# Expert units of layer 0 cut into quarters of 32 rows: 43 units in place of 49

## The chip, the cores and the metric

The kernel runs on one core of a Trainium2 chip. The metric is the time of one execution on the device in microseconds (us), the median of three timed runs. The engines are named as in the profile: PE is TensorE (matmuls), PEld its weight loads, DVE VectorE, ACT ScalarE, POOL GpSimd, SP SyncE; SPq, POOLq and so on are their queues, which issue the transfers.

## What is computed

A two-layer block for 256 context tokens and 256 image tokens with 1024 features. Each layer has a mixer (attention, an mLSTM and an RWKV-7 branch, merged by gates) and then a mixture of experts. All of it is float32. The part that the change touches is the mixture of experts:

```python
def moe_ffn(xf, w_router, router_bias, w_e_gate, w_e_up, w_e_down, w_s_gate, w_s_up, w_s_down):
    scores = jax.nn.sigmoid((xf @ w_router).astype(jnp.float32))
    ...                                  # 64 experts in 8 groups; 4 groups, then 8 experts a token
    _, eidx = lax.top_k(masked, TOP_K)
    wts = wts / (wts.sum(-1, keepdims=True) + 1e-20) * ROUTED_SCALE
    routed = routed_experts(xf, eidx, wts, w_e_gate, w_e_up, w_e_down)
    return routed + swiglu(xf, w_s_gate, w_s_up, w_s_down)

def swiglu(h, w_gate, w_up, w_down):     # 1024 -> 256 -> 1024 for a routed expert
    return (jax.nn.silu(h @ w_gate) * (h @ w_up)) @ w_down
```

In layer 0 all 512 tokens go through it, which makes 4096 pairs of token and expert; in layer 1 only the 256 image tokens, 2048 pairs. Routed with the reference's inputs, the busiest experts of layer 0 get 143, 140, 139, 122, 118, 103 and 94 tokens; those of rank 11 to 28 (counted from 0) get 83 down to 61, and those from rank 29 on get 61 down to 27.

## The kernel before

**Units.** The experts are worked through in units of 128 rows. One unit is: its rows are fetched from DRAM by a gather (`fetch` in `px_pool`, L1594), turned by eight 128x128 transposes (`flip_rows`, L1660), multiplied by the gate and up weights in eight steps of 128 features (`gate_up`, L1670, 512 output columns into one bank), passed through the silu on ACT and DVE (L1772, L1848, L1851), turned again (`flip_hidden`, L1676), multiplied by the down weights (`down`, L1685, two halves of two steps) and written back by a scatter (`store`, L1600). On PE the units are interleaved: gate-up of unit u, the turn of the rows of unit u+1, the down product of unit u-1, the turn of the hidden rows of unit u (`px_pe`).

**What a unit holds.** `Plan` (L43) lays the experts, by how many tokens they have, on positions p of a fixed list of units. A letter F is a unit of one expert (128 rows, weights used at full width, a tile of 128x128 in the array). P is a unit of two experts with 64 rows each: `sides` (L1652) then gives two matmuls for each step, one for output rows 0 to 63, one for 64 to 127, each with a tile of 128x64 in the array and with its own weights as the moving operand. D is a further unit for the last pair of experts, so that each of these has 192 rows. Layer 0 has 30 units of the kind F and 19 of two halves, 49 in all; layer 1 has 34, all of two halves. The last unit of each list is done by a loop (`rest_of`), which also takes what does not fit.

**Weights.** An expert's gate and up weights are 2048 KB and its down weights 1024 KB. There are four places for each; position p uses place p mod 4. SP issues the loads (`px_sync`, L1527 and L1530) in a fixed order: the load for position p waits until the last unit that uses position p-4 has done its gate-up, or its down product. `Plan.loads` holds that order. Layer 0 loads its first four experts once the router has named them.

**The router** (`ro_dve`) computes on DVE in a chain of small operations where each pair of token and expert goes: its row in the units, from `Plan.table`, or a row in the loop's extra blocks of 64 rows.

The program prints here the functions that the diff touches.

Of the kernel before, what the change touches and what calls it, by code (L numbers as in the profile page):

```python
# [7 lines left out]
ALU = mybir.AluOpType  # L8
# [5 lines left out]
P = 128  # L14
L = 2
D = 1024
# [3 lines left out]
T = TC + TX  # L20
TT = T // P
# [20 lines left out]
class Plan:  # L42


    def __init__(self, pinned, order):
        units, blocks, wide, doubled, p = [], {p: [] for p in range(E)}, [], [], 0
        for what in order:
            if what == "F":
                blocks[p] += [(len(units), 0), (len(units), 1)]
                units.append((p, p))  # L50
                wide.append(p)
                p += 1
                continue
            if what == "P":
                p += 2
            else:
                doubled += [p - 2, p - 1]
            blocks[p - 2].append((len(units), 0))
            blocks[p - 1].append((len(units), 1))
            units.append((p - 2, p - 1))  # L60
        assert p == E and units[-1] == (E - 2, E - 1)
        self.pinned, self.all, self.units = pinned, units, units[:-1]
        self.n = len(units) + NOV // 2 + 1
        first = list(range(pinned))
        for some in (doubled, wide, range(E)):
            first += [q for q in some if q not in first]
        self.by_rank, self.blocks = first, blocks
        self.three = any(len(v) > 2 for v in blocks.values())
        last_use = [max(n for n, unit in enumerate(units) if q in unit) for q in range(E)]
        loads = [(last_use[q - 4] + late, last_use[q - 4], kind, q) for q in range(4, E - 2) for kind, late in (("gate_up", 0), ("down", 1.3))]  # L70
        self.loads = [x[1:] for x in sorted(loads, key=lambda x: x[0])]

    def table(self, q):

        v = [P * unit + 64 * half for unit, half in self.blocks[q]]
        return v[0] - P * len(self.all), (v + v[-1:])[1] - v[0], (v[2] - v[1] if len(v) > 2 else 0), len(v)


PLAN = (Plan(0, "FFDP" * 2 + "FFP" * 4 + "P" + "FFP" * 5 + "P" + "FFP" * 4), Plan(4, "PPPDPD" + "P" * 28))
NBLK = max(at.n for at in PLAN)  # L80


# [75 lines left out]
def bcast(ap, axis, n):  # L158

    a = ap.unsqueeze(axis)  # L160
    shape = list(a.shape)
    shape[axis] = n
    return a.broadcast_to(shape)


def build(nc, xin, consts, smalls, wsm, wst, wexp, out):
    es = ExitStack()
    with es:
# [22 lines left out]
        ps = [es.enter_context(nc.psum_tensor(f"bank{i}", [P, 512], F32)) for i in range(8)]  # L191
# [127 lines left out]
        def mod_dve(dve, ch, chunks, bank):  # L319
# [6 lines left out]
            for l, j in chunks:  # L326
                for v, scale in ((0, 8), (1, 32)):
                    if j == scale // 4 + 1:
# [11 lines left out]
                                                      s=32, nm=32, ex=32, pn=32, t=32, pte=32, o=32, oe=4)  # L340
# [954 lines left out]
        def ro_dve(dve, ch, l):  # L1295
            t0 = 0 if l == 0 else TC // P
            n_t = TT - t0
            V = nc.vector
# [42 lines left out]
            at = PLAN[l]  # L1341
            U = len(at.all)
# [6 lines left out]
            ch.link(V.tensor_tensor(r_ties[col, :], r_ties[col, :], cn("before", E)[col, :], ALU.mult))  # L1349
            V.tensor_tensor(r_beats[col, :], r_beats[col, :], r_ties[col, :], ALU.add).then_inc(ro["rk"], 1)  # L1350

            ch.link(V.tensor_scalar(r_pos[:, t0:, :], ps[2][:, t0 * E:TT * E].rearrange("p (t e) -> p t e", e=E), float(P * U), None, ALU.add))
            ch.link(V.tensor_scalar(r_j[:, t0:, :], r_pos[:, t0:, :], 1.0 / BLK, 0.5 / BLK - 0.5 - P * U / BLK, ALU.mult, ALU.add))
            ch.link(V.tensor_scalar(r_j[:, t0:, :], r_j[:, t0:, :], ROUND, None, ALU.add))

            dve.wait_ge(ro["ranked"], l * RO["ranked"] + 1)
            for n in range(4):
# [4 lines left out]
            dve.wait_ge(ro["rk"], l * RO["rk"] + 1)  # L1362
            V.tensor_scalar(r_tab[col, 4, :], ident[col, 0:E], r_n[col, 0:1], None, ALU.mult).then_inc(ro["rk"], 1)
            ch.add(V.tensor_copy(r_incl, ps[3][:, 0:E]))
            ch.link(V.tensor_scalar(r_j[:, t0:, :], r_j[:, t0:, :], ROUND, None, ALU.subtract))
            ch.link(V.scalar_tensor_tensor(r_at[:, t0:, :], r_j[:, t0:, :], -float(BLK), r_pos[:, t0:, :], ALU.mult, ALU.add))

            dve.wait_ge(ro["ranked"], l * RO["ranked"] + 2)
            ch.link(V.tensor_copy(r_row[:, :, :], ps[1][:, 2 * E:7 * E].rearrange("p (a b) -> p a b", b=E)))
            first, second, third, blocks = (r_row[:, n, :] for n in range(4))  # L1370
            dve.wait_ge(ro["rk"], l * RO["rk"] + 2)
            V.tensor_copy(EJI[:, 0:E], r_row[:, 4, :]).then_inc(ro["end"], 1)
            ch.add(V.scalar_tensor_tensor(r_blk[:, t0:, :], r_j[:, t0:, :], 1.0, bcast(second, 1, n_t), ALU.is_ge, ALU.mult))
            ch.link(V.tensor_scalar(r_nov, r_incl, 1.0 / BLK, 0.5 - 0.5 / BLK, ALU.mult, ALU.add))
            ch.add(V.tensor_tensor(r_blk[:, t0:, :], r_blk[:, t0:, :], bcast(first, 1, n_t), ALU.add))
            ch.link(V.tensor_scalar(r_nov, r_nov, ROUND, None, ALU.add))
            if at.three:
                ch.add(V.scalar_tensor_tensor(r_h[:, t0:, :], r_j[:, t0:, :], 2.0, bcast(third, 1, n_t), ALU.is_ge, ALU.mult))
            ch.link(V.tensor_scalar(r_nov, r_nov, ROUND, None, ALU.subtract))
            if at.three:  # L1380
                ch.add(V.tensor_tensor(r_blk[:, t0:, :], r_blk[:, t0:, :], r_h[:, t0:, :], ALU.add))
            ch.link(V.tensor_tensor(r_nov, r_nov, blocks, ALU.subtract))
            ch.add(V.tensor_tensor(r_over[:, t0:, :], r_j[:, t0:, :], bcast(blocks, 1, n_t), ALU.is_ge))
            ch.link(V.tensor_scalar(r_nov, r_nov, 0.0, None, ALU.max))
            ch.add(V.tensor_tensor(r_at[:, t0:, :], r_at[:, t0:, :], r_blk[:, t0:, :], ALU.add))
            ch.link(V.tensor_tensor_scan(out=r_incl, data0=ones[:, 0:E], data1=r_nov, initial=0.0, op0=ALU.mult, op1=ALU.add))
            ch.link(V.tensor_tensor(r_excl, r_incl, r_nov, ALU.subtract))
            ch.link(V.tensor_tensor(r_excl, r_excl, blocks, ALU.subtract))
            ch.link(V.tensor_tensor(r_spill[:, t0:, :], r_j[:, t0:, :], bcast(r_excl, 1, n_t), ALU.add))
            ch.link(V.tensor_scalar(r_h[:, t0:, :], r_spill[:, t0:, :], NOV / 2, 64.0 - P * NOV / 2, ALU.is_ge, ALU.mult))  # L1390
            ch.link(V.scalar_tensor_tensor(r_spill[:, t0:, :], r_spill[:, t0:, :], float(P), r_h[:, t0:, :], ALU.mult, ALU.add))
            ch.link(V.tensor_tensor(r_spill[:, t0:, :], r_spill[:, t0:, :], r_blk[:, t0:, :], ALU.subtract))
# [21 lines left out]
            n = at.n  # L1414
# [231 lines left out]
        def px_pe(pe, l, before):  # L1646
            tiles, at = tiles_of(l), PLAN[l]
            U = len(at.units)
# [2 lines left out]

            def sides(unit):  # L1652

                left, right = unit
                return [(0, P, left)] if left == right else [(0, 64, left), (64, P, right)]

            def flip_rows(s, done, freed=None):
                for h in range(2):
# [32 lines left out]
                flip_rows(u % 4, un["pe"], tl["pe"] if u == U - 1 else None)  # L1691

            def rows_through(u):
                for _, _, p in sides(at.units[u]):
                    pe.wait_ge(gu_in[p % 4], 16 * (loads_past(l, p % 4) + p // 4 + 1))
                if u >= 2:
                    pe.wait_ge(un["dve"], after(l, "dve", "hidden", u - 2))

                def wait_rows(k):
                    if k % 4 == 0:  # L1700
                        eng = ("act", "dve")[k // 4]
                        pe.wait_ge(un[eng], after(l, eng, "rows", u))
                gate_up(at.units[u], u % 2, wait_rows).then_inc(un["pe"], 1)

            def rows_down(u):
                for _, _, p in sides(at.units[u]):
# [17 lines left out]
            rows_down(U - 1)  # L1724

            rest = rest_of(pe, l)
            s, unit = U % 2, (2, 3)
# [466 lines left out]
```

## Time and profile before

| | us |
|---|---|
| median of three runs | 3216.1 |
| lowest and highest | 3215.99, 3217.38 |
| the profiled execution | 3204.1 |
| its span | 3202.2 |
| layer 0, first gate-up to the loop's gate-up | 1132.50 to 1721.31 |
| layer 1, first gate-up to the loop's gate-up | 2626.26 to 3132.42 |

| engine | busy us | share of the span |
|---|---|---|
| PE | 2762.2 | 86% |
| PEld | 1435.7 | 45% |
| DVE | 908.9 | 28% |
| ACT | 624.2 | 19% |
| POOL | 170.7 | 5% |

A row of the timeline says when a run of like instructions starts and how long it takes to the modelled end of the last; the distance from the start of one row to the start of the next is the more exact measure. The chain of waits gives each piece up to the start of the next. PEclk is the granted clock of PE as a share of 2.4 GHz. The program's records count two for each float32 matmul of these shapes, so "x16" is eight matmuls.

### The profile page before, as it was taken

How to read it: one execution, taken by the hardware profiler on the slowest of the kernel's cores; microseconds unless marked ns; L12 is line 12 of the kernel's file. 1: busy time of each engine (PE TensorE's matmuls, PEld its weight loads, DVE VectorE, ACT ScalarE, POOL GpSimd, SP SyncE). 2: the span in 40 equal slices, each digit the busy share in tenths (PEclk: the TensorE clock that was granted, in tenths of full speed). 3: DMA queues.
4: the chain of work that ended last, by engine and by line, in shares of the span. 5: the costliest groups of instructions: out<-in, count | busy, mean ns of one | idle time of the engine just before them, and what ended most of it. 6: DMA issues, size and time to landing. Idle time of an engine off the chain costs nothing.

```text
span 3202.2 us, 38572 instructions
## 1 busy us (share of the span) xinstructions
PE 2762.2 (86%) x15804; PEld 1435.7 (45%) x15804; DVE 908.9 (28%) x1994; ACT 624.2 (19%) x1194; POOL 170.7 (5%) x178
## 2 busy tenths in 40 slices
PE   6868898999999899989898587898989979788885
PEld 3333334765444644434343334343878853233333
DVE  1231454452111622111112412244452142111114
ACT  3231223222001111111110222223222021111111
POOL 0000000000000011111111000000000001111100
PEclk9999568999999699999999699759999979989987
DMA  6000001342210469999996501001223169999994
GB/s 265 33 40 33 0 0 53 134 160 80 79 53 0 190 255 387 418 399 409 370 411 252 232 20 53 33 0 53 82 108 146 65 252 390 424 422 416 415 405 177
DMA packets 74559, 617.37 MB, mean 193 GB/s; under 512 B 17678, under 2 KB 17678, under 8 KB 32016
## 3 DMA queue, kind: packets, MB, share of 16 engines
q1 hardware_dynamic: 50192, 564.52, 43.4%
q0 software_dynamic: 24192, 50.39, 4.2%
q8 instruction: 125, 2.05, 0.3%
q14 instruction: 50, 0.41, 0.0%
HBM read 604.87 MB, written 47.71 MB: 204 GB/s over the span
## 4 chain that ended last, share of the span: by engine, by line
PE 80%; DVE 9%; issue 4%; DMA 3%; ACT 3%; SPq 0%; DVEq 0%; POOLq 0%; ACTq 0%; POOL 0%
PE bank L1670 19%; PE bank L1685 9%; PE bank L1156 8%; PE bank L286 7%; PE bank L356 3%; PE bank L1171 3%; PE bank L1161 3%; PE bank L1660 2%; PE bank L576 2%; PE bank L584 2%; DMA arena<-expert_rows 2%; PE bank L377 1%; PE bank L397 1%; PE bank L874 1%; PE bank L889 1%
## 5 line engine op out<-in xcount | busy, mean ns | idle before, releaser
L1670 PE MATMUL bank<-ring,arena 128*64 128x512 f32 (+1 forms) x1648 | 589.4, 631 | 96.6 <-issue 93.3
L1670 PEld LDWEIGHTS bank<-ring,arena 128*64 128x64 f32 (+1 forms) x1648 | 203.3, 158 | 421.6 <-issue 420.5
L1156 PE MATMUL bank<-normed,ring 128*128 128x512 f32 (+1 forms) x768 | 255.5, 486 | 0.0
L1670 PE MATMUL bank<-branches,arena 128*64 128x512 f32 (+1 forms) x528 | 254.6, 639 | 0.0
L1848 DVE TENSOR_TENSOR arena<-bank,arena 128x256 f32<-128x256 f32 x83 | 35.2, 425 | 702.3 <-ACT arena L1772 702.3
L286 PE MATMUL bank<-normed,ring 128*128 128x512 f32 x512 | 223.4, 598 | 1.3 <-DVE branches L491 1.3
L1594 POOL DMA_INDIRECT arena<-hidden_rows,block_slots x81 | 82.5, 1018 | 2588.8 <-DVE block_slots L1423 1985.3
L1156 PEld LDWEIGHTS bank<-normed,ring 128*128 128x128 f32 x768 | 145.9, 190 | 102.2 <-issue 92.3
L1772 ACT ACTIVATE arena<-bank 128x256 f32<-128x256 f32 x83 | 31.9, 385 | 684.4 <-PE bank L1670 684.4
L1685 PE MATMUL bank<-ring,arena 128*64 128x512 f32 (+1 forms) x560 | 163.4, 597 | 1.3 <-DVE arena L1854 1.3
L286 PEld LDWEIGHTS bank<-normed,ring 128*128 128x128 f32 x512 | 98.0, 192 | 123.9 <-issue 122.1
L1685 PE MATMUL bank<-arena 128*64 128x512 f32 (+1 forms) x528 | 139.9, 604 | 1.1 <-ACT arena L1775 1.1
L1854 DVE COPY arena<-bank 128x512 f32<-128x512 f32 x83 | 57.4, 692 | 223.7 <-PE bank L1685 223.7
L1660 PEld LDWEIGHTS bank<-consts,arena 128*128 128x128 f32 x664 | 73.4, 141 | 64.5 <-issue 59.7
L1600 POOL DMA_INDIRECT expert_rows<-arena,block_slots x81 | 80.7, 996 | 355.9 <-ACT arena L1775 232.5
L356 PE MATMUL bank<-normed,ring 128*128 128x512 f32 x192 | 86.7, 615 | 9.5 <-ACT normed L280 9.5
L1660 PE MATMUL bank<-consts,arena 128*128 128x128 f32 x664 | 89.1, 277 | 5.7 <-DVE arena L1843 3.5
L584 PE MATMUL bank<-arena 128*128 128x256 f32 (+3 forms) x136 | 82.3, 712 | 11.4 <-DVE arena L726 11.0
L1161 PE MATMUL bank<-branches,ring 128*128 128x512 f32 (+1 forms) x256 | 90.4, 486 | 0.0
L1685 PEld LDWEIGHTS bank<-ring,arena 128*64 128x64 f32 (+1 forms) x560 | 55.6, 152 | 77.6 <-issue 77.6
L1670 PEld LDWEIGHTS bank<-branches,arena 128*64 128x64 f32 (+1 forms) x528 | 78.8, 155 | 16.7 <-issue 16.7
L1171 PE MATMUL bank<-arena,ring 128*128 128x512 f32 (+1 forms) x256 | 83.1, 486 | 2.6 <-DVE arena L1200 2.6
(429 smaller groups left out, 3713.1 us busy)
## 6 DMA issues: line engine op xcount, KB each, us to landing
ring<-in_wexp SPq DMA_DIRECT2D x96, 2048.0 KB, 19.3
ring<-in_wst SPq DMA_DIRECT2D x54, 2048.0 KB, 8.5
branches<-in_wexp SPq DMA_DIRECT2D x34, 2048.0 KB, 21.7
ring<-in_wexp SPq DMA_DIRECT2D x66, 1024.0 KB, 21.3
arena<-in_wexp SPq DMA_DIRECT2D x64, 1024.0 KB, 21.8
arena<-expert_rows SPq DMA_DIRECT2D x12, 2048.0 KB, 7.3
ring<-in_wst SPq DMA_DIRECT2D x4, 1536.0 KB, 11.1
hidden_rows<-arena SPq DMA_DIRECT2D x6, 512.0 KB, 2.8
```

Of the source, the lines that this page charges most:

```text
L286: last = nc.tensor.matmul(bank, weights[:, k, j0:j0 + n], H[:, k, :], start=(k == 0), stop=(k == KD - 1))
L356: last = nc.tensor.matmul(ps[j][:, :], w[:, k, (j % 4) * P:(j % 4 + 1) * P], H[:, k, :], start=(k == 0), stop=(k == KD - 1))
L576: nc.tensor.matmul(ps[3 + p % 3][:, j0:j1], zk[q, s * P:(s + 1) * P], zq[q, j0:j1], start=True, stop=True, tile_position=(32 * h, 0)).then ...
L584: nc.tensor.matmul(ps[6 + u % 2][:, j0:j1], VA[:, s, u % MLH, :], Sb[:, p % 2, j0:j1], start=(p in firsts), stop=(p + 1 in firsts or p == ...
L1156: last = nc.tensor.matmul(ps[2 * (n % 4)][:, c0:], wg[:, k, i * P:(i + 1) * P], H[:, k, c0:], start=(k == 0), stop=(k == KD - 1))
L1161: last = nc.tensor.matmul(ps[2 * (n % 4) + 1][:, c0:], wb[:, k, :], BR[:, k, c0:], start=(k == b0), stop=(k == b1 - 1))
L1171: last = nc.tensor.matmul(ps[m % 4][:, c0:], w[:, k, (m % 4) * P:(m % 4 + 1) * P], YM[:, k, c0:], start=(k == 0), stop=(k == KD - 1))
L1594: pool.indirect_dma_start(XG[s], None, hx[l], bass.IndirectOffsetOnAxis(ap=ids_of[:, u, 0:1], axis=0), bounds_check=TOKENS[l] - 1, oob_is_ ...
L1600: pool.indirect_dma_start(yrows[l], bass.IndirectOffsetOnAxis(ap=ids_of[:, u, 1:2], axis=0), YB[s], None, bounds_check=TOKENS[l] * TOPK - ...
L1660: last = nc.tensor.transpose(ps[h][:, k * P:(k + 1) * P], XG[s][:, (4 * h + k) * P:(4 * h + k + 1) * P], ident)
L1670: last = nc.tensor.matmul(ps[2 + s][r0:r1, :], XT_[:, s, k * P + r0:k * P + r1], wt[:, k, :], start=(k == 0), stop=(k == KD - 1))
L1685: last = nc.tensor.matmul(ps[5 + h][r0:r1, :], HDT[:, s, k * P + r0:k * P + r1], wt[:, k, h * 512:(h + 1) * 512], start=(k == 0), stop=(k ...
```

## The change

In `Plan` a unit is now a list of pieces (first row, last row, position), and a piece may have 128, 96, 64 or 32 rows:

- F and P are as before.
- D is two experts in two units: the first has 128 rows in a unit of its own and 32 more (160 in all), the second 96 rows beside those 32.
- T is three experts in two units: 96 rows beside 32, and 96 rows beside 32; the expert in the middle has both pieces of 32 (64 in all).
- Layer 0 is "DPFPT" + "DPPFPT"*3 + "FPT"*2 + "TFP": 43 units, of which 11 have one expert, 14 two halves, and 18 a piece of 96 beside one of 32. By rank there are 4 experts with 160 rows, 7 with 128, 18 with 96 and 35 with 64, 5504 rows in all where there were 6272.
- Layer 1's list gives the same 34 units as before (S stands where D stood).

`sides` cuts a piece of 96 rows into one of 64 and one of 32 for PE, so such a unit has three matmuls for each step: a tile of 128x64 and two of 128x32. The waits for weights go by pieces, the loads by the same rule as before, so that their order follows the new last uses. The router looks up the first row, the rows of the first piece, the jump to the second and the room of each expert, and computes with rows in place of blocks.

```diff
+            elif what == "D":
+                units += [[(0, P, p)], [(0, 96, p + 1), (96, P, p)]]
+                p += 2
+            elif what == "T":
+                units += [[(0, 96, p), (96, P, p + 1)], [(0, 96, p + 2), (96, P, p + 1)]]
+                p += 3
...
-PLAN = (Plan(0, "FFDP" * 2 + "FFP" * 4 + "P" + "FFP" * 5 + "P" + "FFP" * 4), Plan(4, "PPPDPD" + "P" * 28))
+PLAN = (Plan(0, "DPFPT" + "DPPFPT" * 3 + "FPT" * 2 + "TFP"), Plan(4, "PPPSPS" + "P" * 28))
...
             def sides(unit):
 
-                left, right = unit
-                return [(0, P, left)] if left == right else [(0, 64, left), (64, P, right)]
+                return [side for r0, r1, p in unit for side in ([(r0, r0 + 64, p), (r0 + 64, r1, p)] if r1 - r0 == 96 else [(r0, r1, p)])]
```

In the router the three operations on DVE before the rank is known (L1352 to L1354) become one, two more before the table is known (L1365, L1366) go, and the chain behind the table (L1373 to L1394) is written anew: before, 11 operations over all tokens and 8 over the 64 experts in layer 0 (9 and 8 in layer 1); now 17 and 6 in both layers.

```diff
-            ch.link(V.tensor_scalar(r_pos[:, t0:, :], ps[2][:, t0 * E:TT * E].rearrange("p (t e) -> p t e", e=E), float(P * U), None, ALU.add))
-            ch.link(V.tensor_scalar(r_j[:, t0:, :], r_pos[:, t0:, :], 1.0 / BLK, 0.5 / BLK - 0.5 - P * U / BLK, ALU.mult, ALU.add))
-            ch.link(V.tensor_scalar(r_j[:, t0:, :], r_j[:, t0:, :], ROUND, None, ALU.add))
+            ch.link(V.tensor_copy(r_pos[:, t0:, :], ps[2][:, t0 * E:TT * E].rearrange("p (t e) -> p t e", e=E)))
...
+            ch.add(V.tensor_tensor(r_blk[:, t0:, :], r_pos[:, t0:, :], bcast(split, 1, n_t), ALU.is_ge))
+            ch.add(V.tensor_tensor(r_spill[:, t0:, :], r_pos[:, t0:, :], bcast(room, 1, n_t), ALU.subtract))
+            ch.link(V.tensor_tensor(r_nov, r_incl, room, ALU.subtract))
```

On PE, at the second unit of layer 0, before: the turn of the first unit's hidden rows, then the gate-up of unit 1, which is one expert (L1670), the turn of the rows of unit 2 (L1660) and the down product of unit 0 (L1685).

```order
L1676 MATMUL bank4<-consts,arena 128x128 x2
L1670 MATMUL bank3<-ring,arena 128x512 x8
L1660 MATMUL bank0<-consts,arena 128x128 x4
L1660 MATMUL bank1<-consts,arena 128x128 x4
L1685 MATMUL bank5<-ring,arena 128x512 x2
```

The eight full-width matmuls of L1670 stood in one run; the change has another kind of unit in that place.

The same place of the changed program, where the lines are L1671 and L1665; unit 1 is 96 rows of position 1 and 32 of position 0.

```order
L1671 MATMUL bank4<-consts,arena 128x128 x2
L1665 MATMUL bank3<-ring,arena 64x512
L1665 MATMUL bank3<-ring,arena 32x512 x2
L1665 MATMUL bank3<-ring,arena 64x512
L1665 MATMUL bank3<-ring,arena 32x512 x2
```

Each of the eight steps is now one matmul with 64 output rows and two with 32, and the next step's matmul with 64 stands right behind them.

Further on PE, in the changed program, the start of unit 5 (96 rows of position 7, whose weights lie in `branches`, and 32 of position 8): the down product of unit 3, the turn of the hidden rows of unit 4, and two steps of the gate-up.

```order
L1680 MATMUL bank5<-ring,arena 128x512 x2
L1680 MATMUL bank6<-ring,arena 128x512 x2
L1671 MATMUL bank4<-consts,arena 128x128 x2
L1665 MATMUL bank3<-branches,arena 64x512
L1665 MATMUL bank3<-branches,arena 32x512
L1665 MATMUL bank3<-ring,arena 32x512
L1665 MATMUL bank3<-branches,arena 64x512
```

Here too the matmuls alternate between 64 and 32 output rows, the two of 32 being of two experts.

## Rows read from the trace of the kernel before

**Rows 1.** Page: PE's granted clock and DMA over 40 slices of 80 us.

```profile
PEclk9999568999999699999999699759999979989987
GB/s 265 33 40 33 0 0 53 134 160 80 79 53 0 190 255 387 418 399 409 370 411 252 232 20 53 33 0 53 82 108 146 65 252 390 424 422 416 415 405 177
```

**Rows 2.** Chain of waits in order of time, layer 0: start us, us, what.

```profile
1132.50 7.12 PE bank L1670 x16
...
1141.44 6.87 PE bank L1670 x16
...
1362.45 9.68 issue
1372.13 8.83 PE bank L1670 x32
...
1721.31 7.10 PE bank L1670 x32
```

**Rows 3.** Who waited for whom, PE, 1132 to 1722 us: total, times, longest.

```profile
PE bank L1670 <- issue: 21.6, 3, 9.8
```

**Rows 4.** Timeline of PE, three units of layer 0: start us, us, engine, line, what.

```profile
1257.71 0.38 PE L1676 MATMUL bank<-consts,arena 128*128 128x128 f32 x2
1257.93 7.03 PE L1670 MATMUL bank<-ring,arena 128*128 128x512 f32 x16
1264.80 1.04 PE L1660 MATMUL bank<-consts,arena 128*128 128x128 f32 x8
...
1280.80 0.38 PE L1676 MATMUL bank<-consts,arena 128*128 128x128 f32 x2
1281.11 0.64 PE L1670 MATMUL bank<-ring,arena 128*64 128x512 f32 x1
1281.12 0.64 PE L1670 MATMUL bank<-branches,arena 128*64 128x512 f32 x1
...
1288.13 1.09 PE L1660 MATMUL bank<-consts,arena 128*128 128x128 f32 x8
...
1292.71 7.03 PE L1670 MATMUL bank<-ring,arena 128*128 128x512 f32 x16
```

**Rows 5.** Chain of waits, layer 1: a whole unit of two halves.

```profile
2635.18 7.02 PE bank L1670 x32
2643.22 3.58 PE bank L1685 x16
2647.17 7.02 PE bank L1670 x32
```

**Rows 6.** Timeline of PE in layer 0's mLSTM: tiles of 64, 32 and 128 rows.

```profile
376.61 1.91 PE L566 MATMUL bank<-arena,consts 64*128 64x512 f32 x2
378.45 2.07 PE L576 MATMUL bank<-arena 32*128 32x512 f32 x2
380.45 0.80 PE L584 MATMUL bank<-arena 128*128 128x128 f32 x2
381.17 1.64 PE L576 MATMUL bank<-arena 32*128 32x384 f32 x2
...
443.21 1.91 PE L566 MATMUL bank<-arena,consts 64*128 64x512 f32 x2
445.05 2.07 PE L576 MATMUL bank<-arena 32*128 32x512 f32 x2
```

**Rows 7.** Chain of waits, start: a step of the modulation with four groups of 32 columns.

```profile
35.46 1.90 PE bank L303 x16
```

**Rows 8.** A stretch: us, PE busy, granted clock, DMA share, GB/s.

```profile
330.00:345.00 15.00, 15.00 (x21) 0.50 0.00 1
```

**Rows 9.** Timeline of DVE, layer 0: start and end of the chain behind the table.

```profile
1075.51 0.42 DVE L1373 SCALAR_TENSOR_TENSOR arena<-arena 128x256 f32<-128x256 f32 x1
...
1082.16 0.23 DVE L1398 SCALAR_TENSOR_TENSOR arena<-arena 128x64 f32<-128x64 f32 x1
```

**Rows 10.** Page, DMA issues: gate and up weights, KB each, median us to landing.

```profile
ring<-in_wexp SPq DMA_DIRECT2D x96, 2048.0 KB, 19.3
```

More of the change, by code:

```diff
@@ L45, in __init__ @@
     def __init__(self, pinned, order):
-        units, blocks, wide, doubled, p = [], {p: [] for p in range(E)}, [], [], 0
+        units, p = [], 0
         for what in order:
             if what == "F":
-                blocks[p] += [(len(units), 0), (len(units), 1)]
-                units.append((p, p))
-                wide.append(p)
+                units.append([(0, P, p)])
                 p += 1
-                continue
-            if what == "P":
+            elif what == "P":
+                units.append([(0, 64, p), (64, P, p + 1)])
                 p += 2
-            else:
[L57 to L61, printed above, removed]
+            elif what == "D":
[4 more added lines that the diff above has]
+                p += 3
+            else:
+                units.append([(0, 64, p - 2), (64, P, p - 1)])
+        assert p == E and units[-1] == [(0, 64, E - 2), (64, P, E - 1)]
         self.pinned, self.all, self.units = pinned, units, units[:-1]
         self.n = len(units) + NOV // 2 + 1
[L64 to L69, printed above, removed]
+        self.pieces = [[(P * n + r0, r1 - r0) for n, unit in enumerate(units) for r0, r1, q in unit if q == p] for p in range(E)]
+        assert all(len(v) <= 2 for v in self.pieces)
+        self.room = [sum(rows for _, rows in v) for v in self.pieces]
+        self.by_rank = list(range(pinned)) + sorted(range(pinned, E), key=lambda q: -self.room[q])
+        last_use = [max(n for n, unit in enumerate(units) if q in [x[2] for x in unit]) for q in range(E)]
         loads = [(last_use[q - 4] + late, last_use[q - 4], kind, q) for q in range(4, E - 2) for kind, late in (("gate_up", 0), ("down", 1.3))]
@@ L73, in table @@
     def table(self, q):
-        v = [P * unit + 64 * half for unit, half in self.blocks[q]]
-        return v[0] - P * len(self.all), (v + v[-1:])[1] - v[0], (v[2] - v[1] if len(v) > 2 else 0), len(v)
-PLAN = (Plan(0, "FFDP" * 2 + "FFP" * 4 + "P" + "FFP" * 5 + "P" + "FFP" * 4), Plan(4, "PPPDPD" + "P" * 28))
+        (row, rows), *more = self.pieces[q]
+        return row, rows, (more[0][0] - row - rows if more else 0), self.room[q]
+PLAN = (Plan(0, "DPFPT" + "DPPFPT" * 3 + "FPT" * 2 + "TFP"), Plan(4, "PPPSPS" + "P" * 28))
 NBLK = max(at.n for at in PLAN)
@@ L1364, in ro_dve @@
             ch.add(V.tensor_copy(r_incl, ps[3][:, 0:E]))
-            ch.link(V.tensor_scalar(r_j[:, t0:, :], r_j[:, t0:, :], ROUND, None, ALU.subtract))
-            ch.link(V.scalar_tensor_tensor(r_at[:, t0:, :], r_j[:, t0:, :], -float(BLK), r_pos[:, t0:, :], ALU.mult, ALU.add))
             dve.wait_ge(ro["ranked"], l * RO["ranked"] + 2)
             ch.link(V.tensor_copy(r_row[:, :, :], ps[1][:, 2 * E:7 * E].rearrange("p (a b) -> p a b", b=E)))
-            first, second, third, blocks = (r_row[:, n, :] for n in range(4))
+            first, split, jump, room = (r_row[:, n, :] for n in range(4))
@@ L1371, in ro_dve @@
             dve.wait_ge(ro["rk"], l * RO["rk"] + 2)
             V.tensor_copy(EJI[:, 0:E], r_row[:, 4, :]).then_inc(ro["end"], 1)
-            ch.add(V.scalar_tensor_tensor(r_blk[:, t0:, :], r_j[:, t0:, :], 1.0, bcast(second, 1, n_t), ALU.is_ge, ALU.mult))
-            ch.link(V.tensor_scalar(r_nov, r_incl, 1.0 / BLK, 0.5 - 0.5 / BLK, ALU.mult, ALU.add))
-            ch.add(V.tensor_tensor(r_blk[:, t0:, :], r_blk[:, t0:, :], bcast(first, 1, n_t), ALU.add))
-            ch.link(V.tensor_scalar(r_nov, r_nov, ROUND, None, ALU.add))
@@ L1377, in ro_dve @@
[L1377 to L1383, printed above, removed]
@@ L1384, in ro_dve @@
-            ch.link(V.tensor_scalar(r_nov, r_nov, 0.0, None, ALU.max))
+            ch.add(V.tensor_tensor(r_blk[:, t0:, :], r_pos[:, t0:, :], bcast(split, 1, n_t), ALU.is_ge))
+            ch.add(V.tensor_tensor(r_spill[:, t0:, :], r_pos[:, t0:, :], bcast(room, 1, n_t), ALU.subtract))
+            ch.link(V.tensor_tensor(r_nov, r_incl, room, ALU.subtract))
+            ch.add(V.tensor_tensor(r_blk[:, t0:, :], r_blk[:, t0:, :], bcast(jump, 1, n_t), ALU.mult))
+            ch.add(V.tensor_scalar(r_j[:, t0:, :], r_spill[:, t0:, :], 1.0 / BLK, 0.5 / BLK - 0.5, ALU.mult, ALU.add))
@@ L1385, in ro_dve @@
+            ch.link(V.tensor_scalar(r_nov, r_nov, 1.0 / BLK, 0.5 - 0.5 / BLK, ALU.mult, ALU.add))
+            ch.add(V.tensor_tensor(r_at[:, t0:, :], r_pos[:, t0:, :], bcast(first, 1, n_t), ALU.add))
+            ch.add(V.tensor_scalar(r_j[:, t0:, :], r_j[:, t0:, :], ROUND, None, ALU.add))
+            ch.link(V.tensor_scalar(r_nov, r_nov, ROUND, None, ALU.add))
             ch.add(V.tensor_tensor(r_at[:, t0:, :], r_at[:, t0:, :], r_blk[:, t0:, :], ALU.add))
+            ch.add(V.tensor_scalar(r_j[:, t0:, :], r_j[:, t0:, :], ROUND, None, ALU.subtract))
@@ L1386, in ro_dve @@
+            ch.link(V.tensor_scalar(r_nov, r_nov, ROUND, 0.0, ALU.subtract, ALU.max))
+            ch.add(V.tensor_scalar(r_over[:, t0:, :], r_spill[:, t0:, :], 0.0, None, ALU.is_ge))
+            ch.add(V.scalar_tensor_tensor(r_spill[:, t0:, :], r_j[:, t0:, :], -float(BLK), r_spill[:, t0:, :], ALU.mult, ALU.add))
             ch.link(V.tensor_tensor_scan(out=r_incl, data0=ones[:, 0:E], data1=r_nov, initial=0.0, op0=ALU.mult, op1=ALU.add))
-            ch.link(V.tensor_tensor(r_excl, r_incl, r_nov, ALU.subtract))
@@ L1388, in ro_dve @@
[L1388 to L1392, printed above, removed]
+            ch.add(V.tensor_tensor(r_spill[:, t0:, :], r_spill[:, t0:, :], r_at[:, t0:, :], ALU.subtract))
@@ new lines, in ro_dve @@
+            ch.link(V.scalar_tensor_tensor(r_excl, r_incl, float(U), r_nov, ALU.add, ALU.subtract))
+            ch.link(V.tensor_tensor(r_j[:, t0:, :], r_j[:, t0:, :], bcast(r_excl, 1, n_t), ALU.add))
+            ch.add(V.tensor_scalar(r_h[:, t0:, :], r_j[:, t0:, :], NOV / 2 + U, 64.0 - P * NOV / 2, ALU.is_ge, ALU.mult))
+            ch.link(V.scalar_tensor_tensor(r_spill[:, t0:, :], r_j[:, t0:, :], float(P), r_spill[:, t0:, :], ALU.mult, ALU.add))
+            ch.link(V.tensor_tensor(r_spill[:, t0:, :], r_spill[:, t0:, :], r_h[:, t0:, :], ALU.add))
@@ L1693, in rows_through @@
             def rows_through(u):
-                for _, _, p in sides(at.units[u]):
+                for _, _, p in at.units[u]:
                     pe.wait_ge(gu_in[p % 4], 16 * (loads_past(l, p % 4) + p // 4 + 1))
@@ L1705, in rows_down @@
             def rows_down(u):
-                for _, _, p in sides(at.units[u]):
+                for _, _, p in at.units[u]:
                     pe.wait_ge(dn_in[p % 4], 16 * (loads_past(l, p % 4) + p // 4 + 1))
@@ L1726, in px_pe @@
             rest = rest_of(pe, l)
-            s, unit = U % 2, (2, 3)
+            s, unit = U % 2, at.all[-1]
             pe.wait_ge(un["act"], after(l, "act", "out", U - 1))
```

## The prediction

> **What bounds the kernel now.** I read the page's slices first: in layer 0's expert stage, 1132 to 1721 us, PE's clock is near full and DMA already moves 370 to 418 GB/s [rows 1]. The chain of waits through that stage is PE alone, one unit after the other [rows 2], and PE waited for weights there only 21.6 us in three places, one of which is the 9.68 us at 1362.45 [rows 2, 3]. So the stage is PE's, with DMA close behind it. Then I took what a unit costs. In the timeline F, F, P go from the gate-up at 1257.93 to that at 1292.71, 34.78 us [rows 4]. A unit of two halves takes 2647.17 - 2635.18 = 12.0 us [rows 5], so one of the kind F takes (34.78 - 12.0)/2 = 11.4. Check: 30 x 11.4 + 18 x 12.0 = 558 us for the 48 units ahead of the loop; the stage is 1721.31 - 1132.50 = 588.8 [rows 2]. The other 30.8 are 21.6 of waits, some 5 for gate-ups that run slower behind such a wait (8.83 against 7.02 [rows 2, 5]), and 4 at the stage's end.
>
> **What a pair of tiles does.** In the P unit the left half's matmul starts at 1281.11 and the right half's at 1281.12, and the turn of the next rows follows at 1288.13 [rows 4]: two tiles of 128x64 run at the same time. Sixteen matmuls take 7.02 us, where eight of full width take 1264.80 - 1257.93 = 6.87. One step is 6.87/8 = 0.86 us either way. The price of the change of tile shape also stands there: from the last turn to the gate-up 0.31 us in P and 0.22 in F, so 0.09 to go from 128x128 to 128x64, and 7.02 - 6.87 = 0.15 to go back.
>
> **The change part by part.**
>
> *Six units fewer, other kinds.* Ahead of the loop there are now 42 units: 11 F, 13 P and 18 mixed (a piece of 96 beside one of 32). F and P cost as before: 11 x 11.4 + 13 x 12.0 = 281 us. All hangs on the mixed unit, and the trace of before has no matmul of 64 columns beside one of 32, so I bound it from both sides.
>
> *A mixed unit, lower end.* If three tiles (64, 32, 32) ran together like the two halves, it would cost a P unit, 12.0 us. For it speaks that four groups of 32 columns do run together: sixteen records of 512 columns take 1.90 us [rows 7], 0.12 each where one alone takes 0.43. But there all tiles have one shape.
>
> *A mixed unit, upper end.* If PE lets tiles of unlike shape not run together, each step is the matmul of 64 (0.86 us), a change of shape, the two of 32 together (0.86), and a change back. The nearest rows are in the mLSTM. There L566 (a tile of rows 0 to 63) is followed by L576 (a tile of 32 rows), which for heads 2 and 3 is in rows 64 to 127, and writes another bank. Nothing is shared, and the trace shows no wait between the two, yet L576 begins 1.84 us after L566 [rows 6], which is all of L566: 2 x 0.85 at the half clock of that stage [rows 8] is 1.71, and 0.13 on top. All eight passages of layer 0 (four heads, two directions) show the same 1.84, from 376.61 to 378.45 as from 443.21 to 445.05, those with disjoint rows like the others. And two records of 128 columns (2 x 0.21 = 0.43 at half clock) take 381.17 - 380.45 = 0.72 from one change of shape to the next: 0.29 for a change. I can't exclude that row tiles never overlap in this kernel for a reason of their own; that is why the other end keeps a chance. But these are the only rows in which unlike, disjoint tiles follow one another, and in them they do not overlap.
>
> I take the upper end, with the changes of shape at 0.09 and 0.15, which were measured at full clock on columns. A step is then 0.86 x 2 + 0.24 = 1.96 us. Gate-up has eight steps, 15.7; down has four, 7.8; the turns and gaps of a unit are 12.0 - 7.02 - 3.58 = 1.4 [rows 5]. Together 24.9 us, 12.9 more than P. With 0.13 for both changes it is 12 x 1.85 + 1.4 = 23.6, with 0.29 for each 12 x 2.30 + 1.4 = 29.0.
>
> The Trainium skill speaks against the change in the same way: its page "TensorEngine Tiling (Array Packing)", section Tiling Modes, says that tiles work independently, but that changing the tiling mode, "not just tile", drains the engine, and lists 128x64 and 128x32 as two modes. By that rule the mixed unit is the dear one; by rows 7 alone it would be the cheap one. The 1.84 us of rows 6 agree with the rule; no run here yet shows it for columns.
>
> *The sum.* 281 + 18 x 24.9 = 729.6 us, and 4 for the stage's end. DMA needs less than that: an expert's 2048 KB of gate and up weights [rows 10] and half as much for down (3.15 MB) and its share of the gathered and scattered rows (2 x 4096 rows of 4 KB over 64 experts, 0.52 MB) at some 415 GB/s, the fuller slices of [rows 1], are 8.8 us, 60 experts 531 us. So the 21.6 us of waits go, and the slow gate-ups with them. 733.6 - 588.8 = +144.8 us. With the ends of the mixed unit: +121 and +219.
>
> *Loads.* The order of SP's loads follows the last uses. Position 0 is free after unit 1 in place of unit 2, so the first load starts some 11.7 us earlier. With PE as slow as above that gives nothing. If a unit has two new experts beside a neighbour with two, four experts are wanted in 24 us against 35 us of DMA, but the mixed units ahead of them leave DMA time to fill all four places: I count 0 to 3 us.
>
> *Gathers and scatters.* POOL issues six of each fewer, on a queue which nobody waits for; 0. The same rows are moved.
>
> *The router.* The chain behind the table takes 1082.16 - 1075.51 = 6.65 us for 11 wide and 8 narrow operations [rows 9]. With 17 and 6, at some 0.35 for a wide one and 0.25 for a narrow one that isn't hidden in the issue gap of another, I get 7.2 in layer 0, +0.5, and about as much in layer 1; the two operations saved ahead of the rank give 0.2 back in layer 0. PE waits for this chain in both layers. +0.8 us.
>
> *Layer 1's* units are as they were. 0.
>
> Total: 144.8 + 0.8 = +145.6 on the profiled span of 3202.2, 4.5%. The median of the runs is 12 to 14 us above the profiled execution, and I put the same difference on it: 3216.1 + 145.6 = 3361.7.
>
> **The rivals.**
>
> *A: the three tiles run together.* Mixed units cost 12.0, PE needs 281 + 18 x 12.0 = 497 us, and DMA becomes the bound. Its 531 us run from the end of unit 1's gate-up, at 1141.44 + 6.87 = 1148.3 [rows 2], to 1679, if the stream never pauses: -42. In layer 1 the five slices from 2720 us on read 405 to 424 GB/s [rows 1]; there each unit wants two experts, and the stream doesn't pause. In layer 0 units of one and two new experts alternate and it will pause; with 4% of pauses it is 553 us, to 1701: -20. I take -28, 3188. For it: rows 4 and 7. Against it: rows 6.
>
> *B: as A, but the gain is lost* in pauses of the stream and in PE's fall to a lower clock at each wait: with 7% of pauses the stage ends at 1719, within 3 us of now. 3210 to 3219.
>
> *C: tiles don't run together, and the clock falls too.* In 330 to 345 us PE was busy in all of the 15.00 us, with tiles of changing shape, and stayed at 0.50, 1.2 GHz [rows 8], after an idle stretch. If a mixed unit ran at 1.2 GHz it would take some 49 us: up to +570, 3790. Against it: here F and P units, which run at full clock, stand between the mixed ones.
>
> *D: partial overlap,* say the matmul of 64 overlaps one of 32 and not the other, or only one change in two costs. Mixed units of 14 to 22 us, +10 to +100.
>
> *E: the units don't hold the tokens.* Each expert that overflows costs a further round of the loop. By the counts above, no rank has more tokens than room (143 against 160, 118 against 128, 83 against 96, 61 against 64 at the nearest). 1%.
>
> **How the numbers follow.** Forecast (tiles drain at each change of shape, full clock) 0.55, own range 3330 to 3440. A 0.27, B 0.05, C 0.06, D 0.06, E 0.01. The range for 8 in 10 has to hold A and the forecast: 3182 to 3445. It leaves out C and the edges of the others. A measurement of this kernel can tell 0.2%, 6.4 us, from no change. Faster by more: 0.27. Within: 0.05. Slower by more: 0.68.
>
> **What would show it.** In the profile after, the timeline of a mixed gate-up decides: if the matmul of 32 at columns 64 starts 0.01 us behind that of 64, A is right and the gate-up takes 7.0 us; if it starts 0.9 us behind, the forecast is, and it takes 15 to 18. In A PE's waits for weights in the stage grow from 21.6 to some 40 us, and DMA's share is near 1.00; in the forecast they vanish, and GB/s falls to some 320. In C the clock of the stage reads 0.5 to 0.7. The stage from first to last gate-up reads 734 us in the forecast and 550 to 570 in A.

## The result, and the profile after

| | before | after |
|---|---|---|
| median of four runs, us | 3216.05 | 3376.93 |
| lowest and highest | 3212.26, 3217.38 | 3367.73, 3383.49 |
| the profiled execution, and its span | 3204.1, 3202.2 | 3367.7, 3365.9 |
| layer 0, first gate-up to the loop's gate-up | 588.8 | 744.1 |
| from there to layer 1's first gate-up | 905.0 | 910.7 |
| layer 1, first gate-up to the loop's gate-up | 506.2 | 506.1 |

The change makes the kernel slower: the ratio is 1.050, with a 95% interval of 1.0473 to 1.0527. Six units fewer cost 160.9 us by the medians. The prediction was 3361.7 us, with 3182 to 3445 as its range.

The page of the changed kernel first: TensorE's total, its granted clock, and the transfers over 40 slices of 84 us (compare [rows 1]).

```profile
PE 2944.3 (87%) x16344; PEld 1405.7 (42%) x16344; DVE 895.1 (27%) x1970; ACT 612.3 (18%) x1170; POOL 158.1 (5%) x166
...
PEclk9998578999997899999999889958899979998997
...
GB/s 252 69 1 31 0 25 76 114 166 75 75 1 138 192 324 355 267 370 315 335 305 183 245 152 50 7 25 25 94 84 102 125 153 355 421 423 416 417 400 174
```

PE is busy for 2944.3 us where it was 2762.2, and in the full slices of layer 0's stage the transfers run at 267 to 370 GB/s where they ran at 370 to 418. The bytes are the same (617.4 MB), spread over a longer stage: it is PE that has become slower, not the loads.

The chain of waits in order of time, layer 0, after (start us, us, what), answers to [rows 2]:

```profile
1131.31 7.84 PE bank L1665 x16
...
1140.97 15.88 PE bank L1665 x48
...
1161.53 7.02 PE bank L1665 x32
...
1169.57 7.94 PE bank L1680 x24
...
1177.88 6.87 PE bank L1665 x16
...
1868.66 3.69 PE bank L1680 x8
...
1875.38 7.10 PE bank L1665 x32
```

L1665 is the gate-up, L1680 the down product. The number of records names the kind of unit: x16 one expert, x32 two halves, x48 a mixed unit with tiles of 64, 32 and 32 columns. One expert takes 6.87 us and two halves 7.02, as before. The mixed unit takes 15.88, and its down product 7.94. The stage goes from 1131.31 to 1875.38, 744.1 us.

Inside such a gate-up the timeline of PE (start us, us, engine, line, what) shows why:

```profile
1399.43 0.44 PE L1671 MATMUL bank<-consts,arena 128*128 128x128 f32 x2
1399.80 1.62 PE L1665 MATMUL bank<-branches,arena 128*64 128x512 f32 x3
1400.81 0.62 PE L1665 MATMUL bank<-ring,arena 128*32 128x512 f32 x1
1401.26 0.59 PE L1665 MATMUL bank<-branches,arena 128*32 128x512 f32 x1
1401.26 0.59 PE L1665 MATMUL bank<-ring,arena 128*32 128x512 f32 x1
1401.79 1.62 PE L1665 MATMUL bank<-branches,arena 128*64 128x512 f32 x3
```

The tile of 128x64 starts at 1399.80, a tile of 128x32 at 1400.81, 1.01 us later, and the next step's 128x64 at 1401.79. One step is 1.99 us. The two tiles of 32 stand at the same time, 1401.26 both in their second records: they run together, but neither runs with the tile of 64. In the P unit of before, two tiles of 64 started 0.01 us apart [rows 4]. (A row merges records of one line that read the same buffers, whatever their shape. So a row of three records holds the two of the tile of 64 and the first of the tile of 32 of the same expert, which starts together with that of the other expert at 1400.81.)

What PE waited for weights in the stage, after, and two stretches of it (us, busy time of PE, PEld, DVE, ACT and POOL, granted clock, DMA share, GB/s):

```profile
PE bank L1665 <- issue: 4.2, 3, 2.0
```

```profile
1200.00:1300.00 100.00, 100.00 (x342) 25.53 (x341) 17.96 (x85) 9.80 (x20) 10.08 (x10) 1.00 0.73 283
...
1700.00:1800.00 100.00, 100.00 (x348) 25.61 (x344) 11.16 (x21) 10.40 (x21) 9.04 (x9) 1.00 0.73 280
```

The waits are down from 21.6 us [rows 3] to 4.2. In these two stretches PE is busy in every us, and its clock is granted in full (1.00, 2.4 GHz). The DMA engines are idle for a quarter of the time: their share is 0.76 over the whole stage, at 299 GB/s, and 0.73 to 0.90 in single stretches of 100 us from 1200 to 1800; before it was 0.92 over the stage.

The router's chain behind the table, timeline of DVE, first and last operation (compare [rows 9]):

```profile
1072.42 0.42 DVE L1368 TENSOR_TENSOR arena<-arena 128x256 f32<-128x256 f32 x1
...
1079.59 0.23 DVE L1394 SCALAR_TENSOR_TENSOR arena<-arena 128x64 f32<-128x64 f32 x1
```

It takes 7.17 us where it took 6.65.

### The profile page after: what moved, and what is told of

Its sections match the earlier page's. It is cut to its first block, busy times and chain, and to the rows that moved or that the text cites. A ratio compares the mean times of both kernels' runs of the same rounds, so it can differ in the third digit from the quotient of the medians.

```text
span 3365.9 us, 39518 instructions
## 1 busy us (share of the span) xinstructions
PE 2944.3 (87%) x16344; PEld 1405.7 (42%) x16344; DVE 895.1 (27%) x1970; ACT 612.3 (18%) x1170; POOL 158.1 (5%) x166
## 4 chain that ended last, share of the span: by engine, by line
PE 81%; DVE 8%; DMA 4%; issue 4%; ACT 3%; SPq 0%; DVEq 0%; POOLq 0%; ACTq 0%; POOL 0%
PE bank L1665 21%; PE bank L1680 10%; PE bank L1156 7%; PE bank L286 7%; PE bank L356 3%; PE bank L1171 2%; PE bank L1161 2%; PE bank L1655 2%; PE bank L576 2%; PE bank L584 2%; DMA arena<-expert_rows 2%; PE bank L377 1%; PE bank L397 1%; PE bank L889 1%; PE bank L874 1%
## 5 line engine op out<-in xcount | busy, mean ns | idle before, releaser
L1665 PE MATMUL bank<-ring,arena 128*64 128x512 f32 (+2 forms) x1888 | 668.2, 620 | 78.5 <-issue 72.8
L1665 PEld LDWEIGHTS bank<-ring,arena 128*64 128x64 f32 (+2 forms) x1888 | 183.6, 140 | 440.0 <-issue 438.9
L1665 PE MATMUL bank<-branches,arena 128*64 128x512 f32 (+1 forms) x688 | 349.8, 645 | 4.2 <-issue 4.2
L1680 PE MATMUL bank<-ring,arena 128*64 128x512 f32 (+2 forms) x640 | 205.2, 601 | 1.1 <-DVE arena L1849 0.6
L1680 PE MATMUL bank<-arena 128*64 128x512 f32 (+2 forms) x648 | 205.1, 602 | 1.1 <-ACT arena L1770 1.1
L1665 PEld LDWEIGHTS bank<-branches,arena 128*64 128x64 f32 (+1 forms) x688 | 80.5, 138 | 121.3 <-issue 121.3
L1680 PEld LDWEIGHTS bank<-arena 128*64 128x64 f32 (+2 forms) x648 | 50.3, 133 | 109.3 <-issue 109.3
L1680 PEld LDWEIGHTS bank<-ring,arena 128*64 128x64 f32 (+2 forms) x640 | 51.0, 134 | 106.3 <-issue 106.3
## 6 DMA issues: line engine op xcount, KB each, us to landing
ring<-in_wexp SPq DMA_DIRECT2D x96, 2048.0 KB, 15.7
```

What stands on the lines that cost most here:

```text
L1665: last = nc.tensor.matmul(ps[2 + s][r0:r1, :], XT_[:, s, k * P + r0:k * P + r1], wt[:, k, :], start=(k == 0), stop=(k == KD - 1))
L1680: last = nc.tensor.matmul(ps[5 + h][r0:r1, :], HDT[:, s, k * P + r0:k * P + r1], wt[:, k, h * 512:(h + 1) * 512], start=(k == 0), stop=(k ...
```

## The experiments

The theory: tiles of unlike column width don't run together, so a mixed unit pays for two matmuls one after the other and for the changes of shape. The rivals: that something else in the mixed units is dear (the smaller tiles, three matmuls a step, two experts' weights in another order), or that the list, the loads or the router cost the time.

**One shape in a unit.** The changed kernel, with the piece of 96 rows cut into three of 32 in place of 64 and 32. A mixed unit then has four tiles of 128x32, and more matmuls, but no other shape among them.

```diff
-                return [... ([(r0, r0 + 64, p), (r0 + 64, r1, p)] if r1 - r0 == 96 else [(r0, r1, p)])]
+                return [... ([(r, r + 32, p) for r in range(r0, r1, 32)] if r1 - r0 == 96 else [(r0, r1, p)])]
```

> The changed kernel, but a piece of 96 rows is cut into three of 32, so that a mixed unit has four matmuls a step, all with tiles of 128x32, and no change of tile shape inside a unit. Theory (unlike tile shapes drain PE): the four run together as the two halves of 64 do, a mixed gate-up falls from 15.88 us to about 7.0 and its down product from 7.94 to 3.6. PE then needs some 497 us for the stage and DMA becomes the bound: the stage, 744 us in the changed kernel, takes 548 to 569, and the time is 3188 us (3175 to 3200), 1% under the kernel before. Rival (a step with more than two matmuls costs, whatever their shapes: only two streams of data at a time): four matmuls a step need two rounds, the gate-up stays at 14 to 16 us and the time at 3350 to 3390.

Measured: 3192.64 us (3187.10 to 3194.37), ratio to before 0.9931 (0.9915 to 0.9947). The chain, layer 0: the first of these gate-ups, the first long step on weights, and the loop's gate-up.

```profile
1143.86 7.00 PE bank L1665 x64
...
1186.42 18.13 DMA ring<-in_wexp
...
1692.31 7.10 PE bank L1665 x32
```

```profile
PE bank L1665 <- issue: 37.2, 11, 6.4
```

```profile
1200.00:1300.00 100.00, 88.89 (x491) 34.11 (x489) 20.59 (x64) 15.24 (x31) 16.12 (x16) 0.97 1.00 418
1300.00:1400.00 100.00, 92.73 (x540) 34.51 (x542) 14.97 (x28) 13.74 (x28) 14.10 (x14) 0.95 0.99 411
```

The gate-up of a mixed unit falls from 15.88 to 7.00 us with a third more matmuls (x64 records where there were x48). So it is not the smaller size or the larger number of the tiles that costs, it is that they are unlike. The stage is 1692.31 - 1134.91 = 557.4 us, and PE waits 37.2 us for weights while the DMA share reads 0.99 to 1.00: now DMA is the bound, as the prediction's rival A had it for tiles that overlap.

**Changes of shape taken away, the second pass kept.** The changed kernel with its tiles of 64, 32 and 32, but all eight steps of the tile of 64 first, and then all steps of the two of 32; in the down product likewise within each half.

```diff
-                for k in range(KD):
-                    wait_rows(k)
-                    for r0, r1, p in sides(unit):
+                for n, group in enumerate(by_width(unit)):
+                    for k in range(KD):
+                        ...
+                        for r0, r1, p in group:
```

`by_width` sorts the tiles of a unit into groups of one width, wider ones first.

> The changed kernel, but in a mixed unit all eight steps of the tile of 64 go first and all eight of the two tiles of 32 after them, likewise within each half of the down product. The matmuls are the same; the changes of tile shape fall from 16 to 2 in a gate-up and from 8 to 4 in a down product. Theory: nothing overlaps, but the changes go: 2 x 6.87 + 0.3 = 14.0 us for the gate-up in place of 15.88, about 7.4 in place of 7.94 for the down product, 2.4 us for each of 18 units, 43 us in all: 3334 us. Rival (two streams at a time, shape without a part): tiles of 64 and of 32 would now follow without any pairing of unlike ones, the gate-up is 13.7, much the same. This run does not tell the two apart; it gives the price of one change of shape.

Measured: 3335.11 us (3329.75 to 3345.64), ratio 1.0377 (1.0354 to 1.0400). The chain, layer 0: gate-up and down product of mixed units, and the loop's gate-up.

```profile
1147.02 14.00 PE bank L1672 x48
...
1173.74 7.40 PE bank L1688 x24
...
1839.01 7.10 PE bank L1672 x32
```

The gate-up goes from 15.88 to 14.00 with 14 changes of shape fewer: 1.88/14 = 0.134 us a change. The down product goes from 7.94 to 7.40 with four fewer, 0.135 each. So the two parts of the price are apart. Beside a unit of two halves, which has a change at the start and at the end of each product, a mixed unit has 15 changes more in the gate-up and 7 more in the down product: 22 x 0.134 = 2.9 us. The rest of its 13.2 us over such a unit, 10.3, is the lost overlap, 12 steps of 0.86. The 14.00 us are two full passes of 6.87 and 0.26 for the changes at their ends and between them, with nothing of one pass hidden behind the other.

**The mixed shape without the new list.** The kernel before, router, planner and list as they were, but the right half of each unit of two halves in layer 0 is computed as two tiles of 32.

```diff
-                return [(0, P, left)] if left == right else [(0, 64, left), (64, P, right)]
+                return [(0, P, left)] if left == right else [(0, 64, left), (64, 96, right), (96, P, right)] if l == 0 else [(0, 64, left), (64, P, right)]
```

> The kernel before with its own 49 units, and in layer 0 alone the right half (64 rows) of each unit of two halves cut into two matmuls of 32 rows for PE. Same experts, same rows, same weights and transfers; only the tiles are 64, 32, 32 in place of 64, 64. Theory: each of the 19 units gets the 8.9 us on the gate-up and 4.4 us on the down product that the mixed units have, 13.2 us, 251 us in all, less the 21.6 us of waits for weights and some 5 us of slow gate-ups that go: +225 us, 3441 us. Were the cost one of the new list of units, of the pieces that lie in two units or of the loads' order, this kernel would stay at 3216.

Measured: 3444.46 us (3441.51 to 3447.40), ratio 1.0712 (1.0690 to 1.0735). The chain, layer 0, gate-up and down product of such a unit:

```profile
1160.93 15.88 PE bank L1670 x48
...
1198.39 7.94 PE bank L1685 x24
```

The same 15.88 and 7.94 us appear with the old list and the old loads. The stage is 1940.33 - 1140.60 = 799.7 us, 210.9 more than before: 18 units at 13.2 us more, less the 21.6 us of waits and some 5 us of slow gate-ups behind them, which are gone. The 19th such unit is the loop's own, which comes after the stage:

```profile
1940.33 17.54 PE bank L1670 x48
```

The three tiles alone make the cost, wherever they are put.

**The new router without the new tiles.** The changed kernel, with a list for layer 0 that gives the units of before.

```diff
-PLAN = (Plan(0, "DPFPT" + "DPPFPT" * 3 + "FPT" * 2 + "TFP"), ...)
+PLAN = (Plan(0, "FFSP" * 2 + "FFP" * 4 + "P" + "FFP" * 5 + "P" + "FFP" * 4), ...)
```

> The changed kernel with its new router and planner, but with the old list of units for layer 0 (49 units; 4 experts with 192 rows, 26 with 128, 34 with 64), no mixed unit. Theory: all of the loss is in the mixed units; what remains against the kernel before is the router's chain, +0.5 us a layer behind the table, less 0.2 ahead of it: +0.8 us, 3217 us, which a run can't tell from no change. Rival (a part of the 161 us is in the router or elsewhere): 3220 or more.

Measured: 3218.52 us over 12 runs (3209.33 to 3223.43), ratio 1.0007 (0.9996 to 1.0017). PE's waits for weights in its stage are as in [rows 3]:

```profile
PE bank L1665 <- issue: 21.6, 3, 9.7
```

The router with its longer chain and the new planner cost between nothing and 0.2% (up to 5.5 us by the interval; 3.7 us by the medians, that of the kernel before being 3214.8 beside these runs); the expected 0.8 us can't be told from none.

**Fewer bytes.** Is the kernel with one shape in a unit bound by transfers, or by something that merely keeps DMA busy? The same kernel, with half of the down weights left out of the loads of layer 0.

```diff
-            def down(e, w, done):
-                sp.dma_start(DN_W[w], wexp[l, bass.ds(e, 1), :, GU_N:]...)
+            def down(e, w, done, first_use=True):
+                n = D if l == 0 and not first_use else 2 * D
+                sp.dma_start(DN_W[w][:, 0:n], wexp[l, bass.ds(e, 1), :, GU_N:GU_N + n]...)
...
-                    down(e, p % 4, dn_in[p % 4])
+                    down(e, p % 4, dn_in[p % 4], False)
```

> The kernel with four tiles of 32 columns (3192.64 us, stage 557.4 us), but in layer 0 the down weights of the experts at positions 4 to 61 are loaded by half only, the other half of the tile is what the expert before it left; this leaves out part of the weights, so the output is not the reference's. It moves 0.52 MB less for each of 58 experts, 30 MB, some 73 us at the 412 GB/s of that run. Theory (transfers bind that kernel's stage): the stage shortens until TensorE binds it, whose own work in it is some 505 to 515 us by the rows (43 units of 11.4 to 12.0 us), and the waits for weights (37.2 us) go: 3148 us (3140 to 3160). Rival (TensorE or its waits for other things bind it already): 3185 to 3195 us.

Measured: 3137.87 us (3137.81 to 3137.92), ratio 0.9757 (0.9738 to 0.9777). The chain at the first mixed unit and at the loop's gate-up, PE's waits for weights, and one stretch:

```profile
1146.45 7.00 PE bank L1666 x64
...
1641.53 7.10 PE bank L1666 x32
```

```profile
PE bank L1666 <- issue: 3.2, 3, 1.6
```

```profile
1500.00:1600.00 100.00, 100.00 (x658) 37.74 (x661) 19.25 (x36) 17.66 (x36) 15.12 (x15) 1.00 0.97 390
```

The stage is 1641.53 - 1136.84 = 504.7 us, 52.7 less, the waits are 3.2 us, and PE is busy in all of the stretch shown. The bytes taken away (617.48 to 587.08 MB by the pages, 30.4) are 74 us of transfers at 412 GB/s; only 53 are gained, since PE becomes the bound at 505. The prediction's count for PE alone in rival A was 497 us and 4 for the end. The stage came out at the lower end of the 505 to 515 expected, and the time just below the range of 3140 to 3160: it is 54.8 us less than with all the weights, by the medians, where 45 were expected.

**The same units in another order.** One shape in a unit again, and the 43 units listed so that units of two experts stand first and last.

```diff
-PLAN = (Plan(0, "DPFPT" + "DPPFPT" * 3 + "FPT" * 2 + "TFP"), ...)
+PLAN = (Plan(0, "PFPDTPDFPDTFFTPTPFFTDPPTTPFPPPPP"), ...)
```

> The units with four tiles of 32 columns of the run before (3192.64 us, its layer 0 stage 557.4 us, the 16 DMA engines at 0.99 to 1.00 from 1200 to 1600 us but at 0.88 from 1132 to 1200 and 0.91 from 1600 to 1700), and the same 43 units in another order: PFPDTPDFPDTFFTPTPFFTDPPTTPFPPPPP, so that units of two experts stand first and last, and the places for weights come free earlier at the start of the stage. Theory (the stage is bound by the transfer of the weights, and what is left to win is their idle time at its two ends): some 16 us come off the stage, 557 to 541, and the time is 3177 us (3172 to 3188). Rival (the idle share of the DMA engines at the ends is not a matter of the order): no change, 3192 us.

Measured: 3185.27 us (3179.06 to 3188.67), ratio 0.9898 (0.9881 to 0.9915). The stage is 1689.17 - 1142.38 = 546.8 us, 10.6 less than with the other order; 16 were expected. Its first 60 us, its middle and its last 60 us, with the order of the change (the first three rows) and with this one:

```profile
1135.00:1195.00 60.00, 58.16 (x302) 23.72 (x306) 15.15 (x54) 9.21 (x19) 9.99 (x10) 1.00 0.86 350
1195.00:1632.00 437.00, 395.83 (x2322) 151.64 (x2316) 72.56 (x166) 62.78 (x128) 64.45 (x64) 0.96 1.00 412
1632.00:1692.00 60.00, 57.82 (x426) 20.59 (x417) 11.32 (x21) 10.41 (x21) 6.87 (x7) 1.00 0.90 353
```

```profile
1142.00:1202.00 60.00, 59.63 (x288) 24.29 (x290) 14.46 (x44) 9.44 (x20) 10.04 (x10) 0.98 0.96 395
1202.00:1629.00 427.00, 402.46 (x2541) 154.14 (x2535) 75.85 (x178) 64.80 (x132) 65.61 (x65) 0.98 1.00 410
1629.00:1689.00 60.00, 47.55 (x216) 18.62 (x212) 9.35 (x17) 8.45 (x17) 7.33 (x9) 0.96 0.95 392
```

The DMA share of the first 60 us goes from 0.86 to 0.96 and that of the last from 0.90 to 0.95: (0.10 + 0.05) x 60 = 9 us of transfer time regained, about the 10.6. In the middle it was 1.00 and stays so. But the stage ends by definition at the loop's gate-up, and with this order the last load lands just ahead of it:

```profile
1670.85 18.10 DMA branches<-in_wexp
...
1689.17 9.61 PE bank L1665 x32
```

PE waits for that load, and the loop's gate-up takes 9.61 us in place of 7.10. From its start to the load of the experts' rows behind the loop (`arena<-expert_rows` in the chain) it is 22.7 us, with the other order 18.5. So 4.2 of the 10.6 us come back right behind the stage, and 6.4 are left.

This is the fastest of the kernels here that compute the whole. By the medians the order gives 7.4 us; the intervals of the two ratios to before (0.9915 to 0.9947 and 0.9881 to 0.9915) meet at their edge, so the order's gain is likely but small.

## Why the prediction was right

The time is 15.2 us above the 3361.7 predicted, within the range, and the mechanism is the one that was forecast.

**That PE bounds the stage, with DMA close behind:** right. When the mixed units became slow, the stage followed them; when they became cheap, the transfers held the stage at 557 us, 53 above the 505 that it takes with fewer bytes, when PE is the bound.

**The mixed unit, on which all hung:** right. The row on which it rested was a pair of matmuls in another stage, with other rows and another bank, that did not overlap although nothing kept them apart [rows 6]. The traces agree with the rule of the Trainium skill named there (page "TensorEngine Tiling (Array Packing)", section Tiling Modes: a change of the tiling mode drains the engine), for columns too: the runs show 0.134 us for each change between 128x64 and 128x32, and no overlap across it. The step from rows 6 to the mixed unit was an inference all the same, taken at 0.55. In rows 6 the tiles differ in their rows, at half the clock, and no run here tells whether row tiles of one shape would have overlapped in that place; if not, rows 6 gave the right answer by luck. What shows the cause are the runs with four like tiles and with the grouped ones.

**Its size:** 24.9 us was predicted. Measured are 15.88 for the gate-up (15.7), 7.94 for the down product (7.8) and 1.4 for the turns: 25.2. The two changes of a step cost 0.27 together, not the 0.24 taken from [rows 4], which are changes to and from 128x128. The ends of 23.6 and 29.0 held it.

**The sum of the stage:** +144.8 predicted, 744.1 - 588.8 = +155.3 measured. Of the 10.5 us between, 18 x 0.32 = 5.8 are the mixed units, 4.2 the waits for weights, for which the prediction counted 0 to 3 and put nothing into its sum. They stand three times at the same place of the list, where a mixed unit with two new experts follows a unit of two halves. The transfers fell to 299 GB/s, the mean over the stage, where some 320 was named as the sign.

**The router:** +0.5 us for the chain behind the table in layer 0, and 7.17 - 6.65 = +0.52 measured; about as much in layer 1, and there the same distance goes from 4.71 to 5.24. Whether the whole cost is 0.8 lies below what the timing can tell.

**Layer 1's units:** 0 predicted, 506.1 against 506.2 us.

**Outside the stages** nothing was predicted beyond the router, and the profile of after shows +5.7 us between the layers and +4.0 at the end. The router's chain of layer 1 is 0.5 of the 5.7. Between the two stages the profiles take 905.0 us (before), 910.7 (after), and 912.8, 914.7, 919.8, 911.1, 914.1 and 917.1 in the six kernels in the order above. Two of these hold more work of the loop: in the third, with the old router, the loop's unit is mixed too and takes 14.8 us more, and in the last it waits as shown above, 4.2 us. Without that they read 905.1 and 912.9. So the two profiles with the old router read 905 us and the six with the new one 911 to 915. Most of this doesn't lie in the router: a stretch of layer 1's mixer in which PE's instructions are the same in all eight kernels (before, 2240.7 to 2387.4) took 146.6 us before and 148.3 in the other kernel with the old router, 152.7 after, and 151.1 to 155.5 in the rest. Like programs do differ by such amounts: before and the kernel with the mixed shape are the same up to layer 0's stage, and reach it at 1132.50 and 1140.60. But one profile of each kernel doesn't tell chance from an effect of the change on that stretch, and the cause of the 5.7 us stays open. The profiled execution of before lies 12 us below its median and that of after 9 below its own, which is why the profiled spans differ by 163.7 us and the medians by 160.9.

**The rivals.** A (the three tiles together) is wrong for tiles of unlike width and right for equal ones: with four tiles of 32 the stage took 557.4 us, where A had given 550 to 570, and the time was 3192.6, where it had 3188. The pauses that A had placed between the units, where those with one and with two new experts alternate, stood at the two ends of the stage: the share of the DMA engines was 1.00 from 1195 to 1632 us. C (the clock falls) did not come: the granted clock was 1.00 over the whole stage. It was the opposite: the granted clock was 0.95 to 0.98 in the kernel in which PE waits for weights. D (partial overlap) did not come either, and the loop ran no more often than before (E).

## What to carry to other kernels

Count matmuls by tile shape before cutting work into smaller tiles: tiles of equal width ran together up to four at a time, tiles of 64 and of 32 columns not at all, so 96 rows beside 32 go better as four tiles of 32 than as 64, 32 and 32. A plan with fewer units is worth only what the next bound leaves: here PE could have saved 84 us of its stage (588.8 to 504.7), and the transfers let through 31 with one order of the units and 42 with another, of which 4 came back behind the stage; by the medians the whole kernel gained 23 and 31. And for an operation that the trace doesn't show, the nearest row can lie in a quite different stage; two matmuls there, 1.84 us apart without a reason, told more than the case that looked more like it.

## What the runs showed of the hardware

- A change between tiles of 128x64 and 128x32 cost 0.134 us at 2.4 GHz, in gate-up and down product alike, and the matmuls on its two sides did not overlap at all (14.00 us for two passes of eight steps).
- Four tiles of 128x32 with 512 output columns each took 7.00 us for eight float32 steps, where two tiles of 128x64 took 7.02 and one of 128x128 took 6.87. The four times larger number of matmuls cost 0.13 us in 6.87.
- The 16 DMA engines moved 406 to 418 GB/s at a share of 0.99 to 1.00 for 400 us (1200 to 1600 us of the kernel with four like tiles), with PE at work beside them.
- PE's granted clock read 1.00 in the stretches in which it never waited, and 0.95 to 0.98 from 1200 to 1600 us of the kernel with four like tiles. There PE waited for weights eight times (11 in the whole stage), and the gate-ups behind six of these waits took 8.6 to 9.9 us by the chain in place of 7.0.
